# A transformer kernel on one core: the mixers' lower weight parts computed on GpSimd, and the index search moved in the order of the work

## The reference

```python
z = rmsnorm(x, mix_norm) @ w_in
(aq, ak, av, iq, ik, iw, bq, bk, bv, bg, br, cu, dcq, dckv, dkpe) = jnp.split(z, ...)
y_a = dsa_mixer(aq, ak, av, iq, ik, iw, ...)   # attention to the keys that an index selects
y_b = gla_mixer(bq, bk, bv, bg, br, ...)       # gated linear attention
y_c = conv_mixer(cu, ...)                      # gate, 31-tap depthwise convolution, norm, silu
y_d = mla_mixer(dcq, dckv, dkpe, ...)          # latent attention
y = jnp.concatenate([y_a, y_b, y_c, y_d], axis=-1) @ w_out
```

```python
s = jax.nn.relu(jnp.einsum('bthd,bsd->bths', iqb, ik).astype(jnp.float32) * idx_scale)
score = jnp.einsum('bths,bth->bts', s, wb)
score = jnp.where(causal[None], score, -jnp.inf)
_, sel = lax.top_k(score, topk)
```

## Time and profile before

| | |
|---|---|
| median of 3 runs | 4438.09 us (4434.17 to 4439.37) |
| profiled execution | 4426.43 us, of which its span 4425.2 us |
| mean granted TensorE clock | 0.952 |
| PE busy | 4112.5 us, 93% |
| DVE busy | 2267.8 us, 51% |
| ACT busy | 1362.8 us, 31% |
| POOL busy | 149.5 us, 3% |

### The profile page before, as it was taken

One profiled execution on the slowest core, in us unless ns is written; L12 is line 12 of the kernel. 1 busy time (PEld: TensorE's weight loads), 2 busy tenths in 40 slices (PEclk: granted clock), 3 DMA queues, 4 the chain that ended last, 5 costly groups with the idle time before them and its releaser, 6 DMA issues.

```text
span 4425.2 us, 47206 instructions
## 1 busy us (share of the span) xinstructions
PE 4112.5 (93%) x19301; PEld 3236.6 (73%) x19301; DVE 2267.8 (51%) x3544; ACT 1362.8 (31%) x2134; POOL 149.5 (3%) x294
## 2 busy tenths in 40 slices
PE   7659999999999999999999977999999999589999
PEld 6648887666678888887878764788778777467877
DVE  5745898777724444443332488433233325764331
ACT  3243322333333333332221332422232223333221
POOL 8000000000000000000000001000000000100000
PEclk9679999999999999999999986999999999789999
DMA  3002354555566666662333220133323322102332
GB/s 110 1 12 87 110 145 129 164 183 184 183 190 189 190 190 190 190 190 87 95 96 86 62 69 1 53 95 95 100 77 95 96 81 61 46 1 86 95 95 72
DMA packets 253336, 473.56 MB, mean 107 GB/s; under 512 B 15856, under 2 KB 138896, under 8 KB 250944
## 3 DMA queue, kind: packets, MB, share of 16 engines
q1 hardware_dynamic: 253120, 470.53, 35.1%
HBM read 399.96 MB, written 70.52 MB: 106 GB/s over the span
## 4 chain that ended last, share of the span: by engine, by line
PE 79%; DVE 14%; ACT 3%; POOL 2%; issue 1%; DMA 0%; DVEq 0%; ACTq 0%; POOLq 0%; SPq 0%
PE ps L353 23%; PE ps L355 23%; PE ps L354 23%; DVE arena L2656 2%; POOL arena L1139 2%; DVE arena L1825 2%; PE ps L456 1%; PE ps L2223 1%; DVE arena L1139 1%; DVE wlast L344 1%; DVE arena L2751 1%; DVE arena L1821 1%; DVE arena L1822 1%; PE ps L2251 1%; PE ps L2226 1%
## 5 line engine op out<-in xcount | busy, mean ns | idle before, releaser
L344 DVE TENSOR_TENSOR wlast<-wraw,wlast 128x1024 fp32r<-128x1024 f32 x408 | 499.0, 1227 | 799.9 <-ACT wlast L334 799.4
L353 PE MATMUL ps<-XH,wlast 128*128 128x512 f32 (+1 forms) x1904 | 785.4, 412 | 0.7 <-DVE XL L482 0.7
L354 PE MATMUL ps<-XL,wlast 128*128 128x512 f32 (+1 forms) x1904 | 755.4, 397 | 0.0
L355 PE MATMUL ps<-XH,wlast 128*128 128x512 f32 (+1 forms) x1904 | 754.0, 396 | 0.0
L334 ACT ACTIVATE wlast<-wraw 128x1024 fp32r<-128x1024 f32 x408 | 429.4, 1056 | 459.7 <-PE ps L355 444.0
L344 DVE TENSOR_TENSOR wtwo<-wraw,wtwo 128x1024 fp32r<-128x1024 f32 x210 | 258.1, 1230 | 416.9 <-ACT wtwo L334 416.6
L355 PEld LDWEIGHTS ps<-XH,wlast 128*128 128x128 f32 x1904 | 360.3, 189 | 86.5
L353 PEld LDWEIGHTS ps<-XH,wlast 128*128 128x128 f32 x1904 | 360.9, 190 | 74.4 <-issue 3.6
L354 PEld LDWEIGHTS ps<-XL,wlast 128*128 128x128 f32 x1904 | 361.7, 190 | 70.4
L353 PE MATMUL ps<-XH,wtwo 128*128 128x512 f32 (+1 forms) x944 | 383.8, 407 | 0.7 <-DVE XL L482 0.7
L354 PE MATMUL ps<-XL,wtwo 128*128 128x512 f32 (+1 forms) x944 | 368.4, 390 | 0.0
(11 more groups left out here) (460 smaller groups left out, 6542.2 us busy)
## 6 DMA issues: line engine op xcount, KB each, us to landing
wraw<-in_ut SPq DMA_DIRECT2D x128, 512.0 KB, 4.2
wraw<-in_v SPq DMA_DIRECT2D x128, 512.0 KB, 4.0
wraw<-in_ffn_gate SPq DMA_DIRECT2D x88, 512.0 KB, 3.5
wraw<-in_ffn_up SPq DMA_DIRECT2D x88, 512.0 KB, 3.5
wraw<-in_ffn_down SPq DMA_DIRECT2D x88, 512.0 KB, 3.5
acts<-arena SPq DMA_DIRECT2D x128, 256.0 KB, 4.5
gates<-arena SPq DMA_DIRECT2D x16, 2048.0 KB, 9.0
arena<-gates SPq DMA_DIRECT2D x32, 1024.0 KB, 8.3
```

What stands on the lines that cost most here:

```text
L344: ve.e.tensor_tensor(W.items[n][8], W.rawof(n), W.items[n][7], ALU.subtract).then_inc(*ve.up("wlo", n))
L353: mm(out, lh, rh, start=start, stop=False)
L354: mm(out, lh, rl, start=False, stop=False)
L355: return mm(out, ll, rh, start=False, stop=stop)
```

## The change

- `plan_T` and `plan_tok` take a flag, and all 24 projection tiles of a mixer are marked for POOL. `split_ve` passes over them, and a new function, `split_po`, makes their lower parts on POOL. POOL gets a generator for the projections, `po_proj1`, and runs it and `po_index` in the sequence of `order1`.
- Up to the seventh projection, `order1` gives three steps of the index to a projection instead of two, and the scores go through banks 5 to 7 instead of 5 and 6. The first half then ends with 26 steps of `x` issued instead of 21.
- In `order2`, a step of `x` is taken only after more than eight steps of `d`.

```diff
     def add(self, key, src, a, b, group=None, pool=False):
         n = len(self.items)
+        if pool:
+            self.pool.add(n)
...
     while W.split_v < reach(W, key):
         n = W.split_v
-        ve.wait_ge(*at("whi", n))
-        ve.e.tensor_tensor(W.items[n][8], W.rawof(n), W.items[n][7], ALU.subtract).then_inc(*ve.up("wlo", n))
+        if n not in W.pool:
+            ve.wait_ge(*at("whi", n))
+            ve.e.tensor_tensor(W.items[n][8], W.rawof(n), W.items[n][7], ALU.subtract).then_inc(*ve.up("wlo", n))
         W.split_v += 1
+
+
+def split_po(k, key):
+
+    W, po, at = k.W, k.po, k.at
+    while W.split_p < reach(W, key):
+        n = W.split_p
+        if n in W.pool:
+            po.wait_ge(*at("whi", n))
+            po.e.tensor_tensor(W.items[n][8], W.rawof(n), W.items[n][7], ALU.subtract).then_inc(*po.up("wlo", n))
+        W.split_p += 1
...
 def plan_mixer(k, l):
     w2 = k.d[f"w_in2{l}"]
+    T, tok = partial(plan_T, k, pool=True), partial(plan_tok, k, pool=True)
     for m in range(2):
-        plan_T(k, ("iq", l, m), w2, 768 + 128 * m)
...
+        T( ("iq", l, m), w2, 768 + 128 * m)
...
-            for b in "pxxh" if done["p"] < 7 else "pcxch":
+            for b in "pxxxh" if done["p"] < 7 else "pcxch":
...
-                o = k.open(5, 7, "ix", l, i, h)
+                o = k.open(5, 8, "ix", l, i, h)
...
     def po_index(self):
         k, po, at, l = self.k, self.k.po, self.k.at, self.l
         for i in range(1, 4):
+            for _ in range(4):
+                yield
             s = self.SCO[i][:, 128 * i:]
             po.wait_ge(*at("sc", l, i, 7))
...
+    def po_proj1(self):
+        k, l = self.k, self.l
+        for key, n in (("iq", 2), ("ik", 0), ("cu", 4), ("aqk", 512), ("av", 256), ("cq", 2), ("ckv", 0), ("kpe", 0),
+                       ("bv", 256), ("br", 256), ("bq", 0), ("bk", 0), ("bg", 0)):
+            if n >= 256:
+                splits(k, split_po, (key, l), n)
+                yield
+            else:
+                for m in range(max(n, 1)):
+                    split_po(k, (key, l, m) if n else (key, l))
+                    yield
...
-            step("x")
+            if done["d"] > 8:
+                step("x")
...
     def po(self):
         k, l = self.k, self.l
-        self.po_index()
+        x, p = self.po_index(), self.po_proj1()
+        for b in self.order1():
+            if b in "px":
+                next(x if b == "x" else p, None)
         self.po_b()
```

More of the change, by code:

```diff
@@ L253, in __init__ @@
         self.last = self.other("wlast", R)
-        self.items, self.no, self.from0, self.lends = [], {}, 0, []
+        self.items, self.no, self.from0, self.lends, self.pool = [], {}, 0, [], set()
     def other(self, name, dt):
@@ L260, in other, with add @@
             self.k.nc.sbuf_tensor(f"{name}{self.n}", [128, self.LENT * 2048], dt, side="right"))
-    def add(self, key, src, a, b, group=None):
+    def add(self, key, src, a, b, group=None, pool=False):
         n = len(self.items)
+        if pool:
+            self.pool.add(n)
         place = (self.items[-1][4] + 1) % self.PAIRS if n != self.from0 else 0
@@ L298, in walk @@
     def walk(self):
-        self.loaded = self.split_a = self.split_v = 0
+        self.loaded = self.split_a = self.split_v = self.split_p = 0
     def pair(self, key):
@@ L362, in per_tile, with plan_tok @@
     return kk
-def plan_tok(k, key, src, c0, n):
+def plan_tok(k, key, src, c0, n, pool=False):
     kk = per_tile(n)
@@ L368, in plan_tok, with plan_T @@
         k.W.add((key, c), src[128 * kk * c:128 * kk * (c + 1), c0:c0 + n].rearrange("(k p) n -> p k n", p=128),
-                kk, n)
-def plan_T(k, key, src, c0, n=128):
-    k.W.add(key, src[:, c0:c0 + n].rearrange("(k p) n -> p k n", p=128), 8, n)
+                kk, n, pool=pool)
+def plan_T(k, key, src, c0, n=128, pool=False):
+    k.W.add(key, src[:, c0:c0 + n].rearrange("(k p) n -> p k n", p=128), 8, n, pool=pool)
 def pe_tok(k, key, n, lh, ll, tiles, lo=0, hi=8, parts=None):
@@ L2178, in plan_mixer @@
     w2 = k.d[f"w_in2{l}"]
+    T, tok = partial(plan_T, k, pool=True), partial(plan_tok, k, pool=True)
     for m in range(2):
[L2180 to L2181 removed]
+        T( ("iq", l, m), w2, 768 + 128 * m)
+    T( ("ik", l), w2, 1024)
     for m in range(4):
[L2183 to L2185 removed]
+        T( ("cu", l, m), w2, 1848 + 128 * m)
+    tok( ("aqk", l), w2, 0, 512)
+    tok( ("av", l), w2, 512, 256)
     for m in range(2):
[L2187 to L2194 removed]
+        T( ("cq", l, m), w2, 2360 + 128 * m)
+    T( ("ckv", l), w2, 2616)
+    T( ("kpe", l), w2, 2648)
+    tok( ("bv", l), w2, 1320, 256)
+    tok( ("br", l), w2, 1592, 256)
+    T( ("bq", l), w2, 1064)
+    T( ("bk", l), w2, 1192)
+    T( ("bg", l), w2, 1576)
 UNITS = [(i, hp) for i in range(4) for hp in range(2)]
```

12 lines of the change are left out of this document (removed).

## The result

| | before | after |
|---|---|---|
| median | 4438.09 us | 4456.29 us (4449.88 to 4465.97, 5 runs) |
| profiled execution | 4426.43, span 4425.2 | 4450.16, span 4448.9 |
| granted clock, mean | 0.952 | 0.948 |

The ratio is 1.0043 with an interval of 1.0026 to 1.0059: slower by more than the 0.2% that can be told from no change, where 4416 us and faster had been forecast. The range (4384 to 4446) missed it by 10 us.

The account below looks back on a forecast made before the run. PE was busy 93% of the span, with DVE setting the mixers' middle pace. First half +3.3 and second half -14.5 gave -11.2 us a mixer, both -22: from 4438.09 to 4416 us, range 4384 to 4446.

Parts of the forecast that it names:

- part 4: Convolution's stretch: nine splits on POOL hold back DVE's two-input instructions, +12.7 us a mixer, bounds 0 and 15.8.
- part 5: Second half: early search steps leave DVE, -19.1 us; late search partly exposed, +4.6; -14.5 us a mixer.
- cover: Late rounds of the second half: DVE's waits for PE would hide about 4.8 of 9.4 us of late search.
- Part 1: Convolution's stretch: nine splits on the path leave DVE, 10.3 us a mixer less; the other 13 give nothing.
- The lock: Beside the convolution: a POOL split of 1.91 us holds DVE's next two-tensor instruction for 1.75 us.
- the share: Convolution's stretch: the first two splits hold DVE, and three quarters of the seven others.
- slow form: Splits beside the convolution: POOL's subtraction into fp32r is slow, losing from 3.5 us a split on; chance 0.16.
- Part 2: First half: search moved ahead makes the convolution's stretch 2.6 us longer and the half's end 1.2 us shorter.
- Part 3: Index scores in the first half: a third bank spares PE waits for ACT's relu, 1 us, between 0 and 2.8.
- Part 5, middle: Between the halves: without early search steps on DVE, PE's unbroken work begins 19.1 us earlier.
- the latencies take it: Second half: waits double, 9 us gained rather than 16.3, all 9.4 of late search exposed; 4440 us; chance 0.17.
- Part 5, tail: Last rounds of the second half: of 9.4 us of late search on DVE, 4.6 us exposed to PE.

Follow-up runs that it names:

- e1: Kernel before with only the 22 splits of a mixer moved from DVE to POOL; median 4451.08 us, ratio 1.0039.
- e9: Kernel before plus twelve POOL subtractions of 128x1024 at each mixer's start, in four combinations of types, results unused; one execution, 4443.45 us.
- e13: Kernel before plus eight POOL subtractions of 128x768, in four input and output forms, while DVE waits for the gate; one execution, 4430.20 us.
- e2: Changed kernel with all splits back on DVE; 4442.26 us, ratio 1.0018.
- e4: Kernel before with three index steps a projection over three banks; splits on DVE, search not delayed; ratio 1.0015.
- e7: Changed kernel with splits on DVE and the search held back only until the fifth step of the latent attention; ratio 1.0020.
- e11: Changed kernel with splits on DVE, two banks, search held until the fifth latent-attention step, the five additional steps in one block behind the eighth projection; 4451.34 us, ratio 1.0038.
- e12: Changed kernel with splits on DVE, search held back until the fifth latent-attention step, and two banks instead of three; 4455.18 us, ratio 1.0049.
- e10: Kernel before with the index's scores over three banks instead of two, nothing else; ratio 1.0004.
- e3: Kernel before with no search step in the second half until nine latent-attention steps are issued; 4473.0 us, ratio 1.0083.
- e8: Kernel before with the search held back until the fifth step of the latent attention; ratio 1.0061.
- e14: Kernel before with DVE alone doing four search steps ahead of the gate, and the search held back until the fifth latent-attention step; ratio 0.9998.
- e15: Kernel before with DVE alone doing four search steps ahead of the gate, search not held back; ratio 1.0048.
- e5: Kernel before with only the first 15 of a mixer's 24 splits on POOL, those ahead of the convolution; ratio 1.0008.

## Why the forecast was wrong, step by step

The steps that failed are three: the price of a split on POOL beside the convolution (part 4), the clock ahead of the gate, which was put at nothing, and the tail of part 5, whose cover was not there and whose clock was put at nothing. The tail is the largest of them.

**Part 1 (splits off DVE, -10.3).** Right: nine splits of 1.22 us went, 11.0 in all, and e1's stretch is 4.7 us longer with 15.1 us of holding, so their going gave 10.4.

**Part 4 (POOL's splits, +12.7, bounds 0 and 15.8): the term was too small.** It is +17.1 in the changed kernel's first mixer and 15.1 in its second; in e1 it is 15.1 (252 ns on each of 60 instructions) and 17.1. The lock was right, and so was the share: I let 7.25 of the nine splits hold DVE, and seven or eight did. What was too small is the price of one, 1.75 us, where the rows show 2.1. A split takes 2.40 us alone, not 1.91, because the row I took was an instruction with a broadcast factor. The Trainium skill (GPSIMD Engine Reference, Performance versus the Vector engine) gave 2.25, an estimate by half of its 2048-column figure, and was nearer than my row. By that estimate my own sum gives 15.2 us for the nine (2.5 more, not the 2.3 that I wrote). The Trainium skill (SBUF — State Buffer, Who interferes with whom) has the loser stand still for the whole instruction; the 2.90 us of L2671 agree. The rival "slow form" put the price on fp32r as an output and is refuted by e9 and e13.

**Part 2 (order of the steps): right where DVE sets the pace.** The convolution's stretch was to be 2.6 us longer by its other search steps, and is 2.5 us longer in e2, e4, e7, e11 and e12. The 1.2 us saved at the half's end were 0.4 (e2).

**Part 3 (three banks, -1): the lead was there and was lost.** e10's PE is 1.0 and 1.3 us ahead, and its clock takes most of it back.

**The clock ahead of the gate: this I did not see at all.** I took the stretch before the gate as unchanged but for the banks. It is 2.1 and 6.9 us longer in the changed kernel. The size of such a fall, on code that is that of the kernel before, is in e3 and e8: 4.6 and 4.8 us in their second mixers (98.4 to the gate, clock 0.87 and 0.88). With three steps a projection the gate came at 93.8 to 106.5 us in the first mixer and never before 100.4 in the second. With two steps and PE's order that of before it came at 93.5 to 93.9 in the first mixer of ten profiles, and in the second at 93.3 to 93.6 in four and at 98.3 to 100.2 in six.

So part of it is the single execution: e2, e4 and e7 have the same code up to their first gate and reach it at 93.8, 99.0 and 95.7 us. The Trainium skill (TensorE: Matmul & The Clock Gate, What's actually happening) says of a kernel's start that the number of slow matmuls varies between runs of the same kernel; here the place is the middle of a kernel. The profile of before is one whose clock held in both mixers, so the tables above put on the change what a usual execution of before may partly have too. The ratios, which rest on many executions, do not have this fault.

That DVE's work ahead of the gate does not bring the falls is what e14 and e15 show, which have the clocks of e1 and e8 (0.99 or 1.00 / 0.88), whose PE has before's own order; what is left is the order of PE's steps, and e12 (0.78 / 0.77) is its clearest case. By what property of that order the clock falls stays open, since PE is busy equally long at either clock.

The first half's +11.6 in the first mixer adds up like this: 2.1 ahead of the gate, and 9.5 behind it: 10.4 less for the splits that left, 2.5 for the order, 17.1 for POOL, and 0.3 that I can't place.

**Part 5, middle (-19.1): right**, -17.6 and -18.1. The rival "the latencies take it" said -11.8 here (9 and 2.8) and is refuted. Its other half, that none of the late search would be covered, was nearer than my forecast.

**Part 5, tail (+4.6): failed.** The place was right: PE waits 1.90 and 7.60 us in the rows above, for DVE's search of block three and its finish. Over the whole tail it idles 7.6 us more than before, of the 9.4 us of late search, so hardly any of it was covered. The cover of 4.8 I had read off waits of DVE behind its last search step in the kernel before; in the new order DVE is busy 11.3 of each 12 us until 2739, and no wait is left under which to hide. The other 7.4 us are busy time of PE, the clock's. Windows of after, around the wait:

```profile
2739.00:2751.00 12.00, 3.23 (x15) 2.65 (x15) 9.33 (x18) 0.77 (x2) 0.00 (x0) 0.60 0.00 0
2751.00:2763.00 12.00, 12.00 (x41) 8.67 (x41) 2.76 (x8) 3.57 (x13) 0.76 (x3) 0.50 0.01 1
```

and of before, at the same distances from its first scores:

```profile
2745.00:2757.00 12.00, 10.82 (x61) 7.50 (x60) 4.98 (x13) 4.66 (x16) 0.76 (x3) 1.00 0.01 2
2757.00:2769.00 12.00, 12.00 (x61) 7.17 (x61) 3.24 (x8) 5.35 (x17) 1.90 (x5) 1.00 0.00 0
```

Behind its wait PE is busy for all of 12 us at half its clock and does 41 matmuls; the kernel before, at the full clock, did 61. I had added half a microsecond for the clock to the first half and nothing to the tail. That the late search brings the waits is shown by e2 against e4. That it brings the lower clock is not shown to the same degree, since e15 has 0.77 in its tail with six late steps and no more idle time than before.

**The sum.** Forecast -11.2 a mixer: +3.3, -19.1, +4.6. Measured +9.4 and +8.7: of the 20 us between, 8 and 10 are the first half's, 10 and 9 the tail's (first and second mixer), and 1 to 2 the middle's. By ratios, POOL alone costs 0.39%, order and delay 0.18%, all together 0.43%. That is less than the sum, by no more than the intervals allow.

## What to carry to other kernels

Work that is moved out of an engine's busy stretch has to be put into a stretch where that engine waits after the move, not before it: the cover must be counted in the new order. Moving a piece from DVE to POOL is free where the first waits (15 tiles, e5) and a loss where it is busy with two-input instructions (nine tiles, e1), even though the pieces themselves are few. And before a row is taken as the price of an instruction, look up in the code whether both of its inputs are whole tensors; the printed shape does not tell. A profile is one execution: where a stretch runs at a changing clock, a difference of 5 us in 170 between two single profiles (e2 and e4, same code) says nothing about the change.

## What the runs showed of the hardware that I had not expected

- On POOL, a tensor_tensor of 128x1024 takes 1.90 to 1.98 us with one whole tensor to read and 2.34 to 2.40 with two; the output's type (fp32, fp32r) changes nothing.
- POOL and DVE, both with two SBUF inputs, alternate instruction by instruction: 0.74 us becomes 2.83 to 2.90, and 2.40 becomes 2.8.
- PE's granted clock can stay at 0.78 on the mean over 48 us in which PE is busy 45.58 (e12), in the same place in both mixers; it comes with three index steps a projection over two banks, in a half that takes 184.6 us instead of 169.3.
- A third PSUM bank that is worth nothing alone (1.0004) was worth 0.3% beside denser steps (e7 against e12).
- The same 446 matmuls of a tail took PE 79.8, 86.8 and 93.2 us of busy time at mean granted clocks of 0.92, 0.84 and 0.77 (e4, before, e15), with idle times within 0.6 us of each other.
